# The low halves of the projection's weight tiles move from VectorE to GpSimd

## The chip, the cores and the metric

The kernel runs on one core of a Trainium2 chip. The metric is the device time of one execution in microseconds (us). The core has TensorE (PE in the profile), VectorE (DVE), ScalarE (ACT), GpSimd (POOL) and SyncE (SP), which run side by side and wait for each other on semaphores. DMAs are issued from SP and ACT in the part that matters here.

## What is computed

The reference is two transformer blocks over a sequence of 1024 tokens with 1024 channels: a block with an mLSTM and pooling mixer and a mixture of experts, then a block with attention and a dense network. The change is in the mixer of the first block:

```
mod = (silu(c) @ ada_w + ada_b).reshape(bsz, 6, dm)
h = rms_norm(x, norm1_g) * (1 + scale_a) + shift_a
proj = h @ w_in
y_m = mlstm_group(u, v, o_pre, i_pre, f_pre from proj, ...)
y_p = pool_group(p from proj, ...)
mix = concatenate([y_m, y_p]) @ w_out
x = x + gate_a * mix
```

A large product is made of three in a reduced format, fp32r: each factor is split into a high half (the value rounded to fp32r) and a low half (the value less the high half), and high x high, low x high and high x low are added up. So each weight tile needs a copy that rounds, and a subtraction.

## The kernel before

The mixer's projection has 17 weight tiles of 128 columns, numbered n = 0 to 16: four of u, one of the two gates, four of o, four of p (the pooling part), four of v. For each tile PE makes two halves of 512 tokens (`product`), each of 8 x 3 matmuls. The tiles pass through two buffers each: `wb` (the loaded tile, `w_in_tile` in the profile), `wbh` (`w_in_high`) and `wbl` (`w_in_low`).

The way of one tile: ACT issues the load of tile n (`weights(n)`), which waits until the low half of tile n - 2 is made. When both halves of product n - 2 are evacuated, ACT makes the high half (`high(n)`, line 536, semaphore `s_hi`). DVE makes the low half (`low(n)`, lines 759 to 761, semaphore `s_lo`). PE waits for it at the head of product n. In ACT's order the load of tile n + 3 stands between the evacuations of the two halves of product n, so a late low half holds back the second evacuation as well.

Beside this runs the modulation. Ten rows of 1024 values (numbered bundles 0 to 9 here) are each made of 8 pieces of `ada_w` or `w_ada`, 512 KB a piece. Seven of a bundle's pieces are loaded by SP into three rotating buffers (in `v_aug`); DVE adds each, scaled by a value per partition, to `mod_acc` (`piece(j)`, line 757); SP issues piece j when DVE is done with piece j - 3. The eighth (`last_piece(b)`, line 300) goes straight to PE, in the sums (lines 1132 and 1135), which PE makes behind the product named by `summed_in`: bundle 4 behind product 8, bundles 7 and 8 behind products 11 and 12. SP's program has the last piece of a bundle behind the third piece of the next one, so it is issued once DVE has done the first piece of that next bundle.

DVE's program goes tile by tile: for tile n the convolution of tile n - 1 (lines 770 and 773, n = 1 to 4), its share of pieces (`quota`), then `low(n + 2)`, then behind n = 6 the gate rows (`gate_rows`, lines 790 to 803, a chain over 4 x 1024 values with two scans), and from n = 11 on the window sums of the pooling part (`window_sums`, lines 823 to 827, g = 0 to 3). A wait of DVE in `low` therefore stands ahead of everything behind it in that order.

At the end of the stage ACT may not evacuate v tiles 2 and 3 (tiles 15 and 16) before the four window sums are done, since they share memory; behind that evacuation in ACT's order stand the evacuations of the pool products (line 584), for which PE waits (line 1069).

POOL makes the statistics of the norm, then waits for the 16 steps of the convolutions, sets two mask rows for the gate rows (lines 446 and 448, semaphore `r_z`), waits for the sums of all bundles, and multiplies the output weights by the gate (`gated_weights`, line 472).

Of the kernel before, what the change touches and what calls it, by code (L numbers as in the profile page):

```python
# [13 lines left out]
F32 = mybir.dt.float32  # L14
# [4 lines left out]
ALU = mybir.AluOpType  # L19
# [111 lines left out]
def mixer(nc, a, sbuf, sem, psum, bank, ident, ones, mhalf, mods, x1_dram, normed_dram, moe_dram, rows_dram, chosen, picks, first_raw, first_in, masks):  # L131
# [5 lines left out]
    with ExitStack() as ctx:  # L137
# [9 lines left out]
        wb = sbuf(ctx, "w_in_tile", [P, 2, KT, P])  # L147
        wbh = sbuf(ctx, "w_in_high", [P, 2, KT, P], F32R)
        wbl = sbuf(ctx, "w_in_low", [P, 2, KT, P], F32R)
# [38 lines left out]
        s_hi, s_lo, mm, ev, cv, pc, z, s_vt, s_vc, s_sl = [sem("x_" + n) for n in  # L188
            ("w_high", "w_low", "proj", "evac", "conv", "pcol", "const", "v_turned", "v_copied", "silu")]
# [56 lines left out]
        NT = len(tiles)  # L246
# [29 lines left out]
        with nc.Block() as block:  # L276
            @block.sync
            def _(sp):
# [11 lines left out]
                def weights(n):  # L290
                    _, _, at = tiles[n]
                    sp.dma_start(wb[:, n % 2], w_in_pk[:, :, at:at + P]).then_inc(wl[n % 2], 16)
# [130 lines left out]
            def _(pool):  # L423
# [16 lines left out]
                for t in range(TT):  # L440
                    pool.wait_ge(s_sq, t + 1)
                    pool.tensor_scalar(stat[:, t, 0:1], stat[:, t, 0:1], 1.0 / D, EPS, ALU.mult, ALU.add).then_inc(s_e, 1)
                    pool.wait_ge(s_e, t + 1)
                    pool.tensor_tensor(stat[:, t, 1:2], stat[:, t, 0:1], mhalf[:], ALU.pow).then_inc(s_rs, 1)
                pool.wait_ge(cv, 4 * HM)
                pool.memset(rr[:, 3, :], 1.0).then_inc(r_z, 1)
                pool.wait_ge(r_z, 1)
                pool.memset(rr[:, 3, 0:S:P], 0.0).then_inc(r_z, 1)

                def decay_log(c):  # L450
                    d = by_head(de[c % 2])
                    pool.wait_ge(d_neg, 16 * (c + 1))
                    if c >= 2:
                        pool.wait_ge(c_st, c - 1)
                    pool.tensor_tensor(d, by_head(negm), pk[:, c, 0, :].unsqueeze(2).to_broadcast([P, HM, P]), ALU.add).then_inc(c_dl, 1)
                    pool.wait_ge(c_dl, 2 * c + 1)
                    pool.affine_select(out=d, in_=d, compare_op=ALU.is_ge, fill=NEG, base=0,
                                       pattern=[[0, HM], [1, P]], channel_multiplier=-1).then_inc(c_dl, 1)
# [27 lines left out]
                for i in range(TT + 2):  # L486
                    n = i - 2
# [246 lines left out]
            def _(dve):  # L734
# [10 lines left out]
                def piece(j):  # L745
                    b, k = divmod(j, DK)
                    l, q = later[b]
                    dve.wait_ge(s_mp[j % 3], 16 * (j // 3 + 1))
                    if k == 0:
                        dve.wait_ge(s_mb[b % 2], 16 * (b // 2 + 2))  # L750
                        if b >= 2:
                            dve.wait_ge(s_ms, b - 1)
                        added = bt[:, b % 2, :]
                    else:
                        dve.wait_ge(s_ma, j)
                        added = acc[:, b % 2, :]
                    dve.scalar_tensor_tensor(acc[:, b % 2, :], spare[:, j % 3, :], csil[:, l, k:k + 1], added, ALU.mult, ALU.add).then_inc(s_ma, 1)

                def low(n):
                    dve.wait_ge(s_hi, n + 1)  # L760
                    dve.tensor_tensor(wbl[:, n % 2], wb[:, n % 2], wbh[:, n % 2].bitcast(F32), ALU.subtract).then_inc(s_lo, 1)  # L761

                def convolve(m):
                    dve.wait_ge(ev, place[m, 1])
                    for j in range(CW):

                        src = uT[:, m, 0:S - j]
                        tap = pcol[:, 4 * (CW - 1 - j) + m:4 * (CW - 1 - j) + m + 1]
                        if j == 0:
                            dve.tensor_scalar(ucT[:, m, :], src, tap, None, ALU.mult).then_inc(cv, 1)  # L770
                        else:
                            dve.wait_ge(cv, 4 * m + j)
                            dve.scalar_tensor_tensor(ucT[:, m, j:], src, tap, ucT[:, m, j:], ALU.mult, ALU.add).then_inc(cv, 1)

                def copy_values(m):
                    for b in range(2):
                        dve.wait_ge(s_vt, 2 * m + b + 1)
                        dve.tensor_copy(vaug[:, 4 * b:4 * b + 4, m, 0:P], bank[4 + b].rearrange("p (t e) -> p t e", e=P)).then_inc(s_vc, 1)
# [33 lines left out]
                def window_sums(g):  # L812
                    win = 2 << g
                    dve.wait_ge(ev, place[first["p"] + g, 1])
                    if g == 0:
                        dve.wait_ge(r_st, 48)
                    else:
                        dve.wait_ge(p_sum, g)
                    src = pp[:, g, :]
                    for j in range(g + 1):  # L820
                        dst = uT[:, 2 + j % 2, :]
                        sh = 1 << j
                        dve.tensor_copy(dst[:, 0:sh], src[:, 0:sh])
                        then(dve.tensor_tensor(dst[:, sh:], src[:, sh:], src[:, 0:S - sh], ALU.add))
                        src = dst
                    then(dve.tensor_tensor(src[:, 0:16], src[:, 0:16], fix[:, g, :], ALU.mult))
                    dve.scalar_tensor_tensor(pp[:, g, :], src, 1.0 / win, pp[:, g, :], ALU.mult, ALU.subtract).then_inc(p_sum, 1)
# [42 lines left out]
                for n in range(NT):  # L870
                    if 1 <= n <= HM:
                        convolve(n - 1)
                    if n == 5:
                        dve.wait_ge(ev, place[first["g"], 1])
                        dve.wait_ge(cv, 4 * HM)
                        dve.scalar_tensor_tensor(rr[:, 0, :], zf, -1.0, zf, ALU.mult, ALU.max).then_inc(r_abs, 1)
                    for j in range(until[n - 1] if n else 3, until[n]):
                        piece(j)
                    if n + 2 < NT:
                        low(n + 2)  # L880
                    if n == 6:
                        gate_rows()
                    if 0 <= n - first["p"] - 2 < HM:
                        window_sums(n - first["p"] - 2)
                    if first["v"] + 1 <= n:
                        copy_values(n - first["v"] - 1)
# [38 lines left out]
                for i in range(TT + 3):  # L925
                    y, n, lg = i - 1, i - 2, i - 3
# [3296 lines left out]
```

## Time and profile before

| | us |
|---|---|
| three runs | 2495.33, 2497.85, 2503.66 |
| median | 2497.85 |
| profiled execution, its own time | 2499.09 |
| its span, first to last instruction | 2497.5 |
| busy in the span: PE / DVE / ACT / POOL | 2400.2 / 1915.3 / 1354.0 / 590.3 |
| mean granted clock of TensorE | 0.990 |

Times in the rows are us from the start of the span. The projection takes about 60 to 300. A matmul of the products starts some 0.23 us behind the one before it; its own duration in the profile (0.39 us) overlaps the next. "Idle before" is time in which the engine had nothing to do, with what ended it. A row with x3 is three instructions with their total time.

### The profile page before, as it was taken

Reading aid. Unit: us, or ns where it says so; the run is one execution under the profiler, and the core shown is the slowest. Engines: PE = TensorE matmul, PEld = TensorE weight load, DVE = VectorE, ACT = ScalarE, POOL = GpSimd, SP = SyncE. Lnnn points to the kernel's source line nnn. Section 1 sums busy time; section 2 is a strip of 40 time slices with the busy share of each in tenths; the row PEclk is TensorE's granted clock in tenths of the full one; section 3 lists DMA queues with packets and bytes.
Section 4 is the critical chain, followed back from the end, with each engine's and each line's share of the span. In section 5 each row is a group of like instructions: output and inputs, shape, how many; then the busy total and the mean of one; then the engine's idle time right before and its main releaser. Section 6 shows DMA issues by size and latency. Waiting matters only on the chain. (4 is left out here: it accounts for less than half of the span.)

```text
span 2497.5 us, 33891 instructions
## 1 busy us (share of the span) xinstructions
PE 2400.2 (96%) x11969; PEld 1979.8 (79%) x11969; DVE 1915.3 (77%) x2471; ACT 1354.0 (54%) x1924; POOL 590.3 (24%) x492
## 2 busy tenths in 40 slices
PE   7999999899999999999989999999999999999999
PEld 4766678678888887886688999997788888878887
DVE  4876668678989989897877888887766666657786
ACT  3243323357777777775676676776434444444332
POOL 2000444143333233332711111110042333400000
PEclk8999999999999999999999999999999999999999
DMA  6778255589878899998521111113332443587864
GB/s 253 237 246 297 102 208 206 227 318 397 336 270 308 307 398 395 411 394 337 193 69 51 52 52 51 52 39 116 129 110 86 152 167 139 188 314 260 304 252 152
DMA packets 181316, 535.36 MB, mean 214 GB/s; under 512 B 17711, under 2 KB 77715, under 8 KB 167881
## 3 DMA queue, kind: packets, MB, share of 16 engines
q1 hardware_dynamic: 147260, 462.82, 50.6%
q0 software_dynamic: 12592, 45.63, 4.8%
q10 hardware_dynamic: 21340, 25.29, 2.9%
q8 instruction: 75, 1.23, 0.2%
q14 instruction: 49, 0.39, 0.1%
HBM read 443.38 MB, written 90.33 MB: 214 GB/s over the span
## 5 line engine op out<-in xcount | busy, mean ns | idle before, releaser
L1766 PE MATMUL psum<-w_high,block_hT_high 128*128 128x512 f32 x576 | 232.5, 404 | 6.9 <-DVE w_low L1384 5.7
L1384 DVE TENSOR_TENSOR w_low<-first_w_up,w_high 128x2048 fp32r<-128x2048 f32 x72 | 186.5, 2628 | 53.1 <-ACT w_high L1378 53.1
L1768 PE MATMUL psum<-w_high,block_hT_low 128*128 128x512 f32 x576 | 225.3, 391 | 0.0
L1767 PE MATMUL psum<-w_low,block_hT_high 128*128 128x512 f32 x576 | 224.8, 390 | 0.0
L1766 PE MATMUL psum<-w_qkv_high,fox_hT_high 128*128 128x384 f32 (+1 forms) x512 | 181.6, 355 | 8.5 <-DVE w_qkv_low L2613 3.4
L1384 DVE TENSOR_TENSOR w_low<-first_w_gate,w_high 128x2048 fp32r<-128x2048 f32 x74 | 168.6, 2282 | 19.6 <-ACT w_high L1378 19.4
L1766 PE MATMUL psum<-w_mlp_out_high,hidden_part_high 128*128 128x512 f32 x448 | 174.5, 390 | 3.3 <-DVE hidden L4011 1.8
L1480 POOL TENSOR_TENSOR block_out<-block_out,late_rows 128x1024 f32<-128x1024 f32 x35 | 92.7, 2648 | 359.6 <-ACT block_out L1644 359.6
L1378 ACT ACTIVATE w_high<-first_w_gate 128x2048 fp32r<-128x2048 f32 x74 | 141.2, 1912 | 65.4 <-DMA first_w_gate<-in_w_expert_gate 61.6
L1767 PE MATMUL psum<-w_mlp_out_low,hidden_part_high 128*128 128x512 f32 x448 | 174.3, 389 | 0.0
L1768 PE MATMUL psum<-w_mlp_out_high,hidden_part_low 128*128 128x512 f32 x448 | 174.3, 389 | 0.0
L1768 PE MATMUL psum<-w_qkv_high,fox_hT_low 128*128 128x384 f32 (+1 forms) x512 | 173.7, 339 | 0.0
L1767 PE MATMUL psum<-w_qkv_low,fox_hT_high 128*128 128x384 f32 (+1 forms) x512 | 173.7, 339 | 0.0
L1766 PE MATMUL psum<-mix_hT_high,w_in_high 128*128 128x512 f32 x400 | 163.0, 408 | 3.6 <-DVE w_in_low L761 2.1
L1384 DVE TENSOR_TENSOR w_low<-first_w_down,w_high 128x2048 fp32r<-128x2048 f32 x70 | 156.8, 2277 | 2.4 <-ACT w_high L1378 2.4
L1767 PE MATMUL psum<-mix_hT_low,w_in_high 128*128 128x512 f32 x400 | 157.6, 394 | 0.0
L3763 ACT ACTIVATE hidden_part_high<-hidden_part 128x1024 fp32r<-128x1024 f32 x54 | 57.2, 1060 | 175.8 <-PE psum L1768 171.6
L1766 PEld LDWEIGHTS psum<-w_high,block_hT_high 128*128 128x128 f32 x576 | 108.4, 188 | 42.2 <-DVE w_low L1384 19.2
L1378 ACT ACTIVATE w_high<-first_w_down 128x2048 fp32r<-128x2048 f32 x70 | 130.5, 1915 | 19.5 <-DMA first_w_down<-in_w_expert_down 12.8
L1378 ACT ACTIVATE w_high<-first_w_up 128x2048 fp32r<-128x2048 f32 x72 | 133.9, 1915 | 0.6 <-DMA first_w_up<-in_w_expert_up 0.6
L1768 PEld LDWEIGHTS psum<-w_high,block_hT_low 128*128 128x128 f32 x576 | 108.1, 188 | 23.9
L1767 PEld LDWEIGHTS psum<-w_low,block_hT_high 128*128 128x128 f32 x576 | 108.3, 188 | 20.9 <-issue 0.2
(524 smaller groups left out, 6732.3 us busy)
## 6 DMA issues: line engine op xcount, KB each, us to landing
first_w_gate<-in_w_expert_gate SPq DMA_DIRECT2D x32, 2048.0 KB, 10.0
first_w_up<-in_w_expert_up SPq DMA_DIRECT2D x32, 2048.0 KB, 10.4
first_w_down<-in_w_expert_down SPq DMA_DIRECT2D x31, 2048.0 KB, 10.5
w_mlp_out_quarters<-in_w_mlp_out SPq DMA_DIRECT2D x78, 512.0 KB, 7.0
hidden_part<-hidden_parts SPq DMA_DIRECT2D x54, 512.0 KB, 4.4
v_aug<-in_w_ada SPq DMA_DIRECT2D x48, 512.0 KB, 5.1
expert_rows<-block_out POOLq DMA_DIRECT2D x34, 512.0 KB, 8.3
v_aug<-in_ada_w SPq DMA_DIRECT2D x32, 512.0 KB, 4.8
```

The source lines that it names most:

```text
L1378: act.activation(wh[:, par, half], raw[kind][:, half], ACT.Copy).then_inc(s_wh, 1)
L1384: dve.tensor_tensor(wl[:, par, half], raw[kind][:, half], wh[:, par, half].bitcast(F32), ALU.subtract).then_inc(s_wl, 1)
L1480: pool.tensor_tensor(ob[:, u, :], ob[:, u, :], grow, ALU.mult).then_inc(s_om, 1)
L1766: pe.matmul(out, sh, mh, start=start, stop=False)
L1767: pe.matmul(out, sh, ml, start=False, stop=False)
L1768: return pe.matmul(out, sl, mh, start=False, stop=stop)
L3763: act.activation(sph[u][:, ij], h_split(gc, ij), ACT.Copy).then_inc(q_sh, 1)
```

## The change

The low halves of tiles 2 to 16 are written into POOL's program and taken out of DVE's; those of tiles 0 and 1 stay on DVE. In POOL's program tiles 2 to 6 stand ahead of the wait for the convolutions and the mask rows, 7 to 16 behind them, and all ahead of the wait for the sums and of `gated_weights`. PE's, ACT's and SP's programs and all semaphores are the same.

```diff
@@ gpsimd
                     pool.tensor_tensor(stat[:, t, 1:2], stat[:, t, 0:1], mhalf[:], ALU.pow).then_inc(s_rs, 1)
+                def low(n):
+                    pool.wait_ge(s_hi, n + 1)
+                    pool.tensor_tensor(wbl[:, n % 2], wb[:, n % 2], wbh[:, n % 2].bitcast(F32), ALU.subtract).then_inc(s_lo, 1)
+
+                pool.wait_ge(s_lo, 2)
+                for n in range(2, 7):
+                    low(n)
                 pool.wait_ge(cv, 4 * HM)
                 pool.memset(rr[:, 3, :], 1.0).then_inc(r_z, 1)
                 pool.wait_ge(r_z, 1)
                 pool.memset(rr[:, 3, 0:S:P], 0.0).then_inc(r_z, 1)
+                for n in range(7, NT):
+                    low(n)
@@ vector
                     for j in range(until[n - 1] if n else 3, until[n]):
                         piece(j)
-                    if n + 2 < NT:
-                        low(n + 2)
                     if n == 6:
                         gate_rows()
```

POOL between the statistics of the norm and the output weights, before:

```order
L444 TENSOR_TENSOR x_stat<-x_stat,minus_half 128x1
L446 MEMSET yT 4x1024
L448 MEMSET yT 4x8
L475 MEMSET v_aug 128x32
L472 TENSOR_TENSOR mod_acc<-mod_acc,w_in_tile 128x1024 x2
L472 TENSOR_TENSOR mod_bias<-mod_bias,w_in_tile 128x1024 x2
```

and now:

```order
L444 TENSOR_TENSOR x_stat<-x_stat,minus_half 128x1
L447 TENSOR_TENSOR w_in_low<-w_in_tile,w_in_high 128x1024 x5
L453 MEMSET yT 4x1024
L455 MEMSET yT 4x8
L447 TENSOR_TENSOR w_in_low<-w_in_tile,w_in_high 128x1024 x10
L484 MEMSET v_aug 128x32
L481 TENSOR_TENSOR mod_acc<-mod_acc,w_in_tile 128x1024 x2
```

Fifteen subtractions of 128x1024 came in, five ahead of the mask rows and ten between them and the output weights.

DVE around the gate rows, with the modulation pieces (`mod_acc`) of tiles 5 to 7, before:

```order
L757 SCALAR_TENSOR_TENSOR mod_acc<-v_aug,c_silu,mod_acc 128x1024 x6
L761 TENSOR_TENSOR w_in_low<-w_in_tile,w_in_high 128x1024
L757 SCALAR_TENSOR_TENSOR mod_acc<-v_aug,c_silu,mod_bias 128x1024
L757 SCALAR_TENSOR_TENSOR mod_acc<-v_aug,c_silu,mod_acc 128x1024 x5
L761 TENSOR_TENSOR w_in_low<-w_in_tile,w_in_high 128x1024
L790 SCALAR_TENSOR_TENSOR yT<-gate_rows,yT 4x1024
```

and now:

```order
L766 SCALAR_TENSOR_TENSOR mod_acc<-v_aug,c_silu,mod_acc 128x1024 x6
L766 SCALAR_TENSOR_TENSOR mod_acc<-v_aug,c_silu,mod_bias 128x1024
L766 SCALAR_TENSOR_TENSOR mod_acc<-v_aug,c_silu,mod_acc 128x1024 x5
L799 SCALAR_TENSOR_TENSOR yT<-gate_rows,yT 4x1024
```

Low halves 7 and 8 left; the gate rows follow the pieces directly.

DVE between window sums 2 and 3 (`yT`), before:

```order
L826 TENSOR_TENSOR yT<-yT,pool_fix 128x16
L827 SCALAR_TENSOR_TENSOR yT<-yT 128x1024
L761 TENSOR_TENSOR w_in_low<-w_in_tile,w_in_high 128x1024
L823 COPY yT<-yT 128x1
L824 TENSOR_TENSOR yT<-yT 128x1023
```

and now:

```order
L835 TENSOR_TENSOR yT<-yT,pool_fix 128x16
L836 SCALAR_TENSOR_TENSOR yT<-yT 128x1024
L832 COPY yT<-yT 128x1
L833 TENSOR_TENSOR yT<-yT 128x1023
```

The low half of tile 16, and with it DVE's wait for its high half, no longer stands between the two window sums.

## Rows read from the trace of the kernel before

**Rows 1.** Busy time in stretches of 20 us: us, busy (instructions), clock, DMA share, GB/s.
```profile
...
100.00:120.00 20.00, 19.28 (x89) 14.50 (x88) 18.68 (x17) 5.52 (x9) 0.00 (x0) 1.00 0.74 238
...
160.00:180.00 20.00, 16.03 (x65) 10.59 (x63) 16.82 (x16) 7.99 (x9) 0.00 (x0) 0.91 0.51 171
...
200.00:220.00 20.00, 20.00 (x88) 15.02 (x87) 13.63 (x11) 5.29 (x8) 0.00 (x0) 1.00 0.93 323
...
```

**Rows 2.** Waits of PE from 60 to 300: line, for whom, total, times, longest.
```profile
...
PE psum L1132 <- DMA v_aug<-in_w_ada: 6.5, 3, 2.8
PE psum L1069 <- ACT yT L584: 2.1, 1, 2.1
PE psum L1766 <- DVE w_in_low L761: 2.1, 1, 2.1
PE psum L1132 <- DMA v_aug<-in_ada_w: 1.2, 1, 1.2
...
```

**Rows 3.** PE in order of time: start, us, engine, line, names, shapes, count, idle before.
```profile
...
175.57 1.87 PE L1132 MATMUL psum<-v_aug,c_silu 128*1 128x512 f32 x4 [2.81 <-DMA v_aug<-in_w_ada]
...
180.95 0.50 PE L1766 MATMUL psum<-mix_hT_high,w_in_high 128*128 128x512 f32 x1 [2.11 <-DVE w_in_low L761]
...
193.64 1.03 PE L1132 MATMUL psum<-v_aug,c_silu 128*1 128x512 f32 x4
...
196.30 0.48 PE L1766 MATMUL psum<-mix_hT_high,w_in_high 128*128 128x512 f32 x1
...
207.37 1.03 PE L1132 MATMUL psum<-v_aug,c_silu 128*1 128x512 f32 x4
...
209.19 0.50 PE L1766 MATMUL psum<-mix_hT_high,w_in_high 128*128 128x512 f32 x1
...
```

**Rows 4.** DVE in order of time around the low halves and the gate rows.
```profile
...
80.72 1.23 DVE L761 TENSOR_TENSOR w_in_low<-w_in_tile,w_in_high 128x1024 fp32r<-128x1024 f32 x1 [0.71 <-ACT w_in_high L536]
...
126.27 1.23 DVE L761 TENSOR_TENSOR w_in_low<-w_in_tile,w_in_high 128x1024 fp32r<-128x1024 f32 x1 [2.29 <-ACT w_in_high L536]
...
152.28 4.06 DVE L757 SCALAR_TENSOR_TENSOR mod_acc<-v_aug,c_silu,mod_acc 128x1024 f32<-128x1024 f32 x3 [4.23 <-DMA v_aug<-in_w_ada]
156.26 1.22 DVE L761 TENSOR_TENSOR w_in_low<-w_in_tile,w_in_high 128x1024 fp32r<-128x1024 f32 x1
157.39 1.21 DVE L790 SCALAR_TENSOR_TENSOR yT<-gate_rows,yT 4x1024 f32<-4x1024 f32 x1
...
169.24 1.28 DVE L757 SCALAR_TENSOR_TENSOR mod_acc<-v_aug,c_silu,mod_acc 128x1024 f32<-128x1024 f32 x1
...
```

**Rows 5.** SP in order of time: the last piece of bundle 4.
```profile
...
170.92 0.43 SPq L300 DMA_DIRECT2D v_aug<-in_w_ada  x1
...
```

**Rows 6.** POOL, then DVE, in order of time, 261 to 280.
```profile
...
261.69 4.72 POOL L472 TENSOR_TENSOR mod_acc<-mod_acc,w_in_tile 128x1024 f32<-128x1024 f32 x2 [7.97 <-DMA mod_acc<-in_w_out]
266.37 6.71 POOL L472 TENSOR_TENSOR mod_bias<-mod_bias,w_in_tile 128x1024 f32<-128x1024 f32 x2
...
266.25 1.25 DVE L761 TENSOR_TENSOR w_in_low<-w_in_tile,w_in_high 128x1024 fp32r<-128x1024 f32 x1 [5.03 <-ACT w_in_high L536]
...
267.48 3.36 DVE L824 TENSOR_TENSOR yT<-yT 128x1023 f32<-128x1023 f32 x1
270.87 2.23 DVE L823 COPY yT<-yT 128x2 f32<-128x2 f32 x1
...
279.21 1.22 DVE L827 SCALAR_TENSOR_TENSOR yT<-yT 128x1024 f32<-128x1024 f32 x1
...
```

**Rows 7.** POOL writing fp32r, in the stage after the mixer.
```profile
...
496.52 1.74 POOL L1457 TENSOR_TENSOR block_tokens<-block_onehot,token_id 128x384 fp32r<-128x384 f32 x1 [5.76 <-DVE block_onehot L1701]
...
```

**Rows 8.** ACT in order of time: the high half of tile 9, and its late evacuation.
```profile
...
162.41 1.05 ACT L536 ACTIVATE w_in_high<-w_in_tile 128x1024 fp32r<-128x1024 f32 x1
...
280.61 0.60 ACT L562 ACTIVATE yT<-psum 128x512 f32<-128x512 f32 x1 [13.05 <-DVE yT L827]
...
```

**Rows 9.** POOL in order of time: the mask rows.
```profile
...
120.06 0.94 POOL L446 MEMSET yT<- 4x1024 f32 x1 [64.38 <-DVE ucT L773]
...
```

## Prediction

> **What bounds the kernel now.** I read the page first: one core, span 2497.5 us, its own run 2499.09 us, TensorE (PE) busy 96%, and the chain that ended last is PE nearly throughout. So time is won or lost only where PE waits. The change touches one stretch, the projection of the mixer, some 60 to 300 us from the start. The table of stretches [rows 1] shows PE busy nearly all of 100:120 but 16.03 of 20 us in 160:180, at a mean granted clock of 0.91, with the DMA engines at 0.51 there against 0.74. VectorE (DVE) is busy 18.68 of 20 us in 100:120. The list of waits [rows 2] then names what PE lacks: 6.5 us (3 times) and 1.2 us for the DMA of a modulation piece ("last piece", used by the sums), 2.1 us once for a low half made by DVE, 2.1 us once for ScalarE's (ACT's) evacuation of a pool product at the end of the stage. The low halves as such cost PE only one wait of 2.11 us.
>
> PE in order of time [rows 3]: the sums of bundle 4 stand at 175.57 after 2.81 us of waiting for the piece, and product 9 begins at 180.95 after another 2.11 us for its low half. Sums take 209.19 - 207.37 = 1.82 us where PE is warm; here 180.95 - 2.11 - 175.57 = 3.27 us. Product 9 lasts 193.64 - 180.95 = 12.69 us against 207.37 - 196.30 = 11.07 for product 10, so 1.6 us go to the half clock (1.2 of 2.4 GHz) that the idle time left behind.
>
> Why the last piece is late: DVE [rows 4] makes low 8 at 156.26, then the gate rows from 157.39 to 169.24, and only then the first piece after them, which ends at 170.52; SP issues the last piece at 170.92 [rows 5], 4.65 us before PE has it. That chain, DVE to SP to DMA to PE, is what the change moves.
>
> **Step 1, the work leaves DVE.** 15 low halves (tiles 2 to 16) go. One is 1.22 us, and costs DVE 157.39 - 156.26 = 1.13 us in a row [rows 4]. DVE also loses the waits that it makes only for a high half: 0.71 us before low 2 and 2.29 before low 6 [rows 4], and 5.03 before low 16 [rows 6]. The same 15 go to GpSimd (POOL), which did almost nothing there. One multiplication of this shape takes POOL 4.72 / 2 = 2.36 us with DVE silent [rows 6]. The output type (fp32r) isn't in that row; the only POOL row that writes it took 1.74 us for 384 columns [rows 7], beside a DVE instruction. By columns that bounds it at 1.74 x 1024 / 384 = 4.6 us; the lower end is 2.3. I take 2.36, since the inputs and shape are those of that row. Either is far inside the time that a product lasts, so the low half is ready before PE wants it: the high half of tile 9 ends at 162.41 + 1.05 = 163.46 [rows 8], its low half would at 165.8, PE wants it near 179.
>
> **Step 2, the price: the two engines exclude each other.** Where POOL multiplies at 266.37 (two, 6.71 us instead of 4.72), DVE's addition at 267.48 takes 3.36 us instead of 1.22, and a copy of two columns at 270.87 takes 2.23 us [rows 6]. So each POOL instruction holds DVE's next one back by 3.36 - 1.22 = 2.14 us if DVE has work, and by nothing if DVE waits for a DMA; DVE gets one instruction in between. A low half that cost DVE 1.13 us now costs it 0 to 2.14.
> The Trainium skill, "SBUF — State Buffer", section "Who interferes with whom", says the same as a rule: a VectorE instruction with two SBUF inputs and a GpSimd one that reads SBUF need one port, and whoever comes second blocks for the whole instruction. By that rule the change could be a loss on DVE wherever DVE is busy; the trace agrees, with the 2.14 us above.
>
> Up to 127 us DVE is the busy one. Five low halves (2 to 6): 5 x (2.14 - 1.13) = +5.0 us, less the waits 0.71 + 2.29 = -3.0, leaves +2.0; DVE's short waits for pieces take up part of it, I take +1.2. From 127 to 157 the pieces wait for their loads (4.23 us before the one at 152.28 [rows 4]); low 7 and 8 leave, -2.26, and the POOL low 8 (ready at about 149.3) falls into that very wait; but pieces that wait for loads give only part of this back. I take -1.9 with half a block of +0.9 for low 7, net -1.0. Low 9 (163.46) falls into the gate rows, two-input instructions in a chain: +2.14. Some of it overlaps the instruction already running: +1.1 to +2.14. Together the last piece of bundle 4 is issued 1.2 - 1.0 + 1.1 = +1.3 us later. Bounds: -3 (all blocks hidden, only the saved waits) to +9.2 (8 full blocks, 8 x 2.14 = 17.1, less 7 x 1.13 = 7.9, nothing else given back).
>
> **Step 3, what PE gets.** At product 9: the sums begin 1.3 us later, 176.9, last 3.3, product 9 begins at 180.1 instead of 180.95: -0.8. The wait for the low half (2.11) goes, the wait for the piece grows. Less idle time, so perhaps less half clock: of the 1.6 us I count half, -0.8 (0 to -1.6). At the sums of the two later bundles that wait, PE loses the other 6.5 - 2.81 = 3.7 us [rows 2, 3]. There DVE is busy only 13.63 of 20 us [rows 1]: it waits for loads itself, so 1.13 us less work per tile brings little: -0.3 (-3.7 if these waits go, +1.3 if the delay of the last piece is carried on).
>
> **Step 4, the end of the stage.** Window sum 3 ends at 279.21 + 1.22 = 280.43 [rows 6]. Before it DVE waited from 261.22 to 266.25, 5.03 us, for the last high half, then made low 16; then POOL's multiplications by the gate blocked it three times. ACT waited 13.05 us for it [rows 8], and PE 2.1 us for ACT [rows 2]. In the new order, window sum 3 follows window sum 2 at once, at 261.2. It took 280.43 - 267.4 = 13.0 us, 6.6 without the three blocks; with two blocks (low 15 or 16 and one multiplication) it is 10.9, so it is done by 272.1 even if nothing before it is earlier; ACT then evacuates tile 15 as soon as PE has made it. The 2.1 us go: -2.1. Cover gone? POOL now starts to multiply the output weights by the gate after low 16, at about 268.6 instead of 261.69: five times 2.36 to 3.36 us (6.71 / 2), done by 281 to 286. ACT takes them up only when product 16 is done, two half products (11.07 us) and more behind the 280.61 of [rows 8]: hidden. The mask rows, a memset of 0.94 us at 120.06 [rows 9], come after low 6, about 129, and are needed by the gate rows at 157: hidden.
>
> **Sum.** -0.8 - 0.8 - 0.3 - 2.1 = -4.0 us on 2499.09: 2495.1. That execution is 1.24 us above the median of the three runs (2497.85), which would be 2493.9; I say 2494.5. Behind the mixer nothing changes, and PE's chain carries the shift to the end.
>
> **Rivals.**
> A, forecast: as above, 2494.5.
> B, the blocks hide nearly all: then the last piece comes 2.2 us earlier (low 7 and 8), the 2.11 goes, the half clock goes (1.6), the later waits halve (-1.9), one of the slow sums there becomes a warm one (3.27 - 1.82 = -1.5), and step 4 stays: -2.2 - 2.1 - 1.6 - 1.9 - 1.5 - 2.1 = -11.4, so 2487. For it: DVE is idle a third of the time once past the gate rows [rows 1]. Against: in 100:120 it is busy 93%, and the gate rows have no gaps.
> C, slower: the port. If DVE is held by full blocks up to the gate rows and gets nothing back, the last piece is 9.2 us late. Product 9 then begins 9.2 - 2.1 = 7.1 us later; less the 2.1 of step 4 that is +5.0. The later loads follow the same DVE and keep the delay, and the waits behind them grow by as much as they are now (+3.7): +8.7, 2507. It decides from a delay of the last piece above 4.2 us (2.11 + 2.1). A POOL instruction of 4.6 us leads here too. For it: 18.68 of 20 [rows 1]; against: DVE waits for loads between 127 and 157, where delay is taken up.
> D, the change does little: the piece chain gets as late as the low half was (+2.1) and step 4 is the only gain: 2497.
> The Trainium skill, "GPSIMD Engine Reference", section "3.1 Elementwise — side-by-side cycle accounting", puts a two-input GpSimd operation at about twice VectorE's time and keeps elementwise work on VectorE. The rows say 2.36 against 1.22. By that rule alone the move is wrong; it becomes a loss only through the blocks, which is C.
>
> **Numbers.** A 0.55, D 0.15, B 0.18, C 0.12. A change of 0.3% (7.5 us) is about what a measurement of this kernel can tell from none; the three runs shown differ by 8.3 us. A and D lie within it, 0.70, with 0.03 of B and 0.02 of C: same 0.75, faster 0.15, slower 0.10. The range 2487 to 2502 leaves out C and the best of B; A's own is 2490 to 2498.
>
> **What the new profile would show.** Step 1: w_in_low written by POOL 15 times at 2.4 to 3.5 us, no wait of PE for it. Step 2: DVE pieces, convolutions and gate rows with single durations of 2.5 to 3.5 us in place of 1.2, about one for each POOL low; the gate rows ending at 170 to 171. Step 3: the last piece of bundle 4 issued near 172, PE's wait for it 3 to 5 us. Step 4: no wait of PE for ACT at the pool products, window sum 3 done before 273. I am wrong if PE's waits for pieces rise above 12 us in the stage (then C), or vanish (B), or if a POOL low takes over 4 us alone.

## The result

The changed kernel took 2508.59 us (median of 9 runs, 2494.24 to 2516.26), the kernel before 2497.85 us (9 runs, 2492.85 to 2504.61). The ratio is 1.0040, 95% interval 1.0023 to 1.0057: slower by 0.4%, a difference clear of zero, where 2494.5 and "no change to be told" were forecast. The time is just above rival C's 2507.

The profiled execution of the changed kernel took 2507.42 us, its span 2505.8, so 8.3 us more than before on both. The place is the projection. As its length I take the time from DVE's low half of token tile 5 to the first query/key matmul of PE: 299.83 - 63.05 = 236.8 us before, 308.83 - 61.44 = 247.4 changed (both rows are below). That is +10.6; the execution began that stretch 1.6 us earlier and the rest of the span is 0.7 us shorter.

Waits of PE in the changed kernel from 60 to 300 (line, for whom, total, times, longest), beside [rows 2]:

```profile
PE psum L1139 <- DMA v_aug<-in_w_ada: 12.3, 4, 3.5
PE psum L1139 <- DMA v_aug<-in_ada_w: 6.2, 2, 4.5
```

The waits for a low half and for ACT's evacuation are gone, as forecast. The waits for last pieces grew from 7.7 to 18.5 us.

Busy time in stretches of the changed kernel (columns as in [rows 1]):

```profile
100.00:120.00 20.00, 15.48 (x63) 10.18 (x62) 18.47 (x14) 4.29 (x7) 2.82 (x1) 0.83 0.65 214
160.00:180.00 20.00, 17.52 (x78) 14.17 (x76) 18.44 (x15) 8.37 (x10) 2.47 (x1) 1.00 0.43 142
200.00:220.00 20.00, 20.00 (x88) 14.74 (x87) 13.22 (x10) 5.42 (x8) 3.09 (x1) 0.95 0.82 277
```

In 100:120, where PE was busy 19.28 of 20 us before, it is now busy 15.48, at a granted clock of 0.83. In 160:180 it is busier than before (17.52 us, 16.03 in [rows 1]): there the gain at product 9 shows. In 200:220 it is busy throughout, as before, at a transfer share of 0.82 instead of 0.93. The first of the three stretches is ahead of the gate rows and of every wait of PE that the forecast reckoned with.

PE in order of time in the changed kernel, beside [rows 3]: the sums of bundles 1, 4, 5, 7 and 8, the heads of products 4, 9 and 14, and the first query/key matmul:

```profile
...
112.10 1.87 PE L1139 MATMUL psum<-v_aug,c_silu 128*1 128x512 f32 x4 [4.52 <-DMA v_aug<-in_ada_w]
...
116.99 0.48 PE L1773 MATMUL psum<-mix_hT_high,w_in_high 128*128 128x512 f32 x1
...
180.22 1.03 PE L1139 MATMUL psum<-v_aug,c_silu 128*1 128x512 f32 x4 [2.71 <-DMA v_aug<-in_w_ada]
...
182.53 0.80 PE L1773 MATMUL psum<-mix_hT_high,w_in_high 128*128 128x512 f32 x1
...
197.82 1.20 PE L1139 MATMUL psum<-v_aug,c_silu 128*1 128x512 f32 x4 [3.04 <-DMA v_aug<-in_w_ada]
...
229.73 1.87 PE L1139 MATMUL psum<-v_aug,c_silu 128*1 128x512 f32 x4 [3.50 <-DMA v_aug<-in_w_ada]
...
247.26 1.87 PE L1139 MATMUL psum<-v_aug,c_silu 128*1 128x512 f32 x4 [3.10 <-DMA v_aug<-in_w_ada]
...
264.78 0.50 PE L1773 MATMUL psum<-mix_hT_high,w_in_high 128*128 128x512 f32 x1
...
308.83 1.06 PE L1192 MATMUL psum<-ucT,query_key 128*128 128x128 f32 x8
...
```

The first wait is 4.52 us at bundle 1. The sums and transposes behind it run at the half clock (granted 0.50 in 112:116, against 1.00 in 109:114 before): from 112.10 to the next product 4.89 us, against 112.70 - 109.29 = 3.41 before. Then come bundles 3 (1.63, before 1.17), 4 (2.71, before 2.81), 5 (3.04, before none), 7 (3.50, before 2.66) and 8 (3.10, before 1.08).

To see why bundle 1 is late, DVE, SP and PE in the kernel before: the start of the stretch, a convolution, a piece, the issue of the last piece of bundle 1, its sums and the product behind them, DVE's first instruction on the gates' tile, the head of product 14 and the end of the stretch:

```profile
...
63.05 1.22 DVE L743 TENSOR_TENSOR mix_hT_low<-psum,mix_hT_high 128x1024 fp32r<-128x1024 f32 x1
...
82.65 3.92 DVE L773 SCALAR_TENSOR_TENSOR ucT<-yT,param_cols,ucT 128x1023 f32<-128x1023 f32 x3
...
91.42 1.28 DVE L757 SCALAR_TENSOR_TENSOR mod_acc<-v_aug,c_silu,mod_acc 128x1024 f32<-128x1024 f32 x1 [0.87 <-DMA v_aug<-in_ada_w]
...
102.83 0.43 SPq L300 DMA_DIRECT2D v_aug<-in_ada_w  x1
...
109.29 1.03 PE L1132 MATMUL psum<-v_aug,c_silu 128*1 128x512 f32 x4
...
112.70 0.48 PE L1766 MATMUL psum<-mix_hT_high,w_in_high 128*128 128x512 f32 x1
...
127.42 1.20 DVE L876 SCALAR_TENSOR_TENSOR yT<-gate_rows 4x1024 f32<-4x1024 f32 x1
...
253.42 0.50 PE L1766 MATMUL psum<-mix_hT_high,w_in_high 128*128 128x512 f32 x1
...
299.83 1.06 PE L1185 MATMUL psum<-ucT,query_key 128*128 128x128 f32 x8
...
```

and in the changed kernel DVE at the same places and around the gate rows, then SP's issues of the last pieces of bundles 1, 4, 5 and 7:

```profile
...
61.44 1.22 DVE L752 TENSOR_TENSOR mix_hT_low<-psum,mix_hT_high 128x1024 fp32r<-128x1024 f32 x1
...
79.40 5.94 DVE L782 SCALAR_TENSOR_TENSOR ucT<-yT,param_cols,ucT 128x1023 f32<-128x1023 f32 x3
...
85.26 3.42 DVE L766 SCALAR_TENSOR_TENSOR mod_acc<-v_aug,c_silu,mod_bias 128x1024 f32<-128x1024 f32 x1
...
93.33 1.28 DVE L766 SCALAR_TENSOR_TENSOR mod_acc<-v_aug,c_silu,mod_acc 128x1024 f32<-128x1024 f32 x1 [1.87 <-DMA v_aug<-in_ada_w]
...
95.31 5.95 DVE L782 SCALAR_TENSOR_TENSOR ucT<-yT,param_cols,ucT 128x1023 f32<-128x1023 f32 x3
...
129.61 1.22 DVE L885 SCALAR_TENSOR_TENSOR yT<-gate_rows 4x1024 f32<-4x1024 f32 x1 [2.84 <-ACT gate_rows L578]
...
159.98 1.21 DVE L799 SCALAR_TENSOR_TENSOR yT<-gate_rows,yT 4x1024 f32<-4x1024 f32 x1
...
168.54 2.78 DVE L807 TENSOR_SCALAR yT<-yT 4x1024 f32<-4x1024 f32 x1
...
105.64 0.43 SPq L300 DMA_DIRECT2D v_aug<-in_ada_w  x1
...
175.61 0.43 SPq L300 DMA_DIRECT2D v_aug<-in_w_ada  x1
...
190.37 0.43 SPq L300 DMA_DIRECT2D v_aug<-in_w_ada  x1
...
222.28 0.43 SPq L300 DMA_DIRECT2D v_aug<-in_w_ada  x1
...
```

Three convolution steps together take 5.94 and 5.95 us instead of 3.92, and a piece 3.42 instead of 1.28: three blocks of 2.0 to 2.1 us, one for each of the POOL subtractions of low 2, 3 and 4, which start at 79.23, 84.69 and 95.48. SP issues the last piece of bundle 1 at 105.64 - 61.44 = 44.2 us into the stretch instead of 102.83 - 63.05 = 39.8, and PE has it 6.46 us after the issue.

The rows also show which piece sets these issues. SP's program has the last piece of a bundle behind the load that waits for the bundle's own seventh piece (for bundle 4 the one at 169.24 in [rows 4]; the next bundle's first piece, with `mod_bias` among its inputs, starts only at 170.44), not behind DVE's first piece of the next bundle. The times read from the rows stay the same.

### The profile page after: what moved, and what is told of

It is laid out like the page before. It is cut to its first block and busy times, and to the rows that moved or that the text cites. A ratio compares the mean times of both kernels' runs of the same rounds, so it can differ in the third digit from the quotient of the medians.

```text
span 2505.8 us, 33892 instructions
## 1 busy us (share of the span) xinstructions
PE 2402.1 (96%) x11969; PEld 1978.4 (79%) x11969; DVE 1915.9 (76%) x2456; ACT 1354.6 (54%) x1924; POOL 636.0 (25%) x507
## 6 DMA issues: line engine op xcount, KB each, us to landing
first_w_gate<-in_w_expert_gate SPq DMA_DIRECT2D x32, 2048.0 KB, 10.3
first_w_up<-in_w_expert_up SPq DMA_DIRECT2D x32, 2048.0 KB, 10.2
```

## The experiments

Each kernel from memset_low on ran in five rounds beside the kernel before. In the four series (that of the result and three more) the median of the kernel before was 2497.85, 2498.29, 2499.67 and 2498.49 us; kernels of different series are best compared by their ratios. "Issue 1", "issue 4" and "issue 8" are the issues of the last pieces of bundles 1, 4 and 8 in the profiled execution, in us from the start of the stretch; "stretch" is its length. Each kernel has one profiled execution, so how far a stretch repeats is not measured; I don't read differences of under 2 us in it. The rest of the span, behind and ahead of the stretch, varies more: from 2253.4 us (after_b1) to 2267.8 (two_tiles), in no order that follows the edits. So a difference of a few us in the time need not lie in the stretch. Up to bundle 1 the traces repeat: issue 1 is 39.8 or 39.9 in all eight kernels that leave low halves 2 to 6 on DVE without extra POOL work.

| kernel | median us | ratio to before (95%) | issue 1 | issue 4 | issue 8 | stretch |
|---|---|---|---|---|---|---|
| before | 2498 | | 39.8 | 107.9 | 168.6 | 236.8 |
| changed | 2508.6 | 1.0040 (1.0023 to 1.0057) | 44.2 | 114.2 | 178.3 | 247.4 |
| memset_low | 2494.6 | 0.9991 (0.9977 to 1.0006) | 36.9 | 105.0 | 166.9 | 236.1 |
| extra_blocks | 2510.8 | 1.0059 (1.0042 to 1.0077) | 45.8 | 117.8 | 180.0 | 250.4 |
| late_tiles | 2499.8 | 1.0011 (0.9996 to 1.0026) | 39.8 | 109.2 | 170.8 | 236.0 |
| early_tiles | 2504.6 | 1.0017 (1.0001 to 1.0034) | 44.2 | 111.7 | 172.2 | 242.2 |
| two_tiles | 2499.1 | 0.9995 (0.9979 to 1.0012) | 39.8 | 108.8 | 170.9 | 236.2 |
| late_tiles_loads | 2497.8 | 0.9986 (0.9970 to 1.0002) | 39.8 | 108.5 | 172.0 | 238.1 |
| early_last | 2503.0 | 1.0030 (1.0013 to 1.0047) | 42.5 | 96.5 | 173.9 | 246.0 |
| after_b1 | 2504.1 | 1.0018 (1.0005 to 1.0032) | 42.7 | 114.0 | 176.2 | 241.5 |
| two_tiles_b4 | 2501.1 | 0.9998 (0.9980 to 1.0016) | 39.9 | 91.7 | 169.7 | 237.6 |
| inter_before | 2495.9 | 0.9993 (0.9981 to 1.0005) | 39.8 | 96.4 | 165.8 | 235.2 |
| inter_two | 2496.4 | 0.9987 (0.9973 to 1.0001) | 39.9 | 96.5 | 167.3 | 234.8 |
| inter_late | 2494.3 | 0.9984 (0.9969 to 0.9998) | 39.8 | 96.8 | 168.2 | 237.0 |

**memset_low: the change without GpSimd's reads.**

```diff
-                    pool.tensor_tensor(wbl[:, n % 2], wb[:, n % 2], wbh[:, n % 2].bitcast(F32), ALU.subtract).then_inc(s_lo, 1)
+                    pool.memset(wbl[:, n % 2].bitcast(F32), 0.0).then_inc(s_lo, 1)
```

> The changed kernel, but GpSimd fills the low halves of tiles 2 to 16 with zero (a memset, which reads nothing) instead of subtracting, so the product lacks that term. Order, semaphores and the early release of the tile buffers stay. Stage length is measured from VectorE's low half of token tile 5 to the first query/key matmul: 236.8 us before, 247.4 changed. Theory P (the port: GpSimd's reads hold VectorE, so the pieces, and with them SP's issue of the last pieces, come late): single durations of pieces and convolutions back at 1.28 us, stage 228 to 234 us, PE's waits for pieces 5 to 10 us (18.5 in the changed kernel), time 2484 to 2493. Theory L (loads: with the tile buffers released earlier, the loads of the w_in tiles collide with those of the pieces): stage stays 244 to 249, time as changed, near 2508.

Measured: 2494.6 us, 14 under the changed kernel; stretch 236.1. A POOL memset and a convolution beside it, a piece, the issue of the last piece of bundle 1, a gate row with one input, then a tile load of ACT, the last piece of bundle 5 and PE's wait for it:

```profile
...
79.94 1.16 POOL L447 MEMSET w_in_low<- 128x1024 f32 x1 [25.21 <-ACT w_in_high L545]
...
80.24 3.92 DVE L782 SCALAR_TENSOR_TENSOR ucT<-yT,param_cols,ucT 128x1023 f32<-128x1023 f32 x3
...
88.82 1.28 DVE L766 SCALAR_TENSOR_TENSOR mod_acc<-v_aug,c_silu,mod_acc 128x1024 f32<-128x1024 f32 x1 [0.68 <-DMA v_aug<-in_ada_w]
...
99.10 0.43 SPq L300 DMA_DIRECT2D v_aug<-in_ada_w  x1
...
161.38 1.53 DVE L807 TENSOR_SCALAR yT<-yT 4x1024 f32<-4x1024 f32 x1
...
179.47 0.55 ACTq L554 DMA_DIRECT2D w_in_tile<-in_w_in  x1
...
181.68 0.96 SPq L300 DMA_DIRECT2D v_aug<-in_w_ada  x1
...
189.63 1.87 PE L1139 MATMUL psum<-v_aug,c_silu 128*1 128x512 f32 x4 [4.77 <-DMA v_aug<-in_w_ada]
...
```

The convolutions are back at 3.92 us and issue 1 stands at 36.9, 7.3 us earlier than in the changed kernel and 2.9 earlier than before. So the loss comes with POOL's reads, as theory P says, and not with the early tile loads, which this kernel has too. But P also asked for 2484 to 2493 and a stretch of 228 to 234, and that missed. DVE is rid of 15 low halves almost free of price (a gate row with one input, the row at 161.38, still takes 1.53 us instead of 0.68), and the median is 3.7 us lower, with an interval from 5.7 us lower to 1.5 higher. In its trace product 9 begins 6.4 us earlier than before (111.52 us into the stretch, before 117.90), and product 14 begins 1.7 us later (192.10, before 190.37): with no block at all, a lead of 6.4 us at the gate rows is spent on waits for pieces behind them. PE waits 4.77 us at bundle 5 for a piece issued at 181.68, 7.95 us before, just behind a tile load.

**extra_blocks: the price alone.** The kernel before with 13 POOL subtractions that nobody needs, for tiles 2 to 6 ahead of the mask rows and for 7 to 14 behind them; DVE still makes every low half:

```diff
+                def block(n):
+                    pool.wait_ge(s_hi, n + 1)
+                    pool.tensor_tensor(sq[64:P, :], hTh[64:P, 0, :].bitcast(F32), hTl[64:P, 0, :].bitcast(F32), ALU.subtract).then_inc(s_junk, 1)
```

> The kernel before, its low halves on VectorE, plus 13 GpSimd subtractions of 64 partitions x 1024 from tensors that don't change, each at the time of the high half of tiles 2 to 14, into an unused place. Theory P: each holds VectorE up to 2.1 us on top of the 1.13 us that it still spends on the low half; stage 248 to 256 us, PE waits at the sums of bundles 1, 4, 7 and 8, time 2509 to 2518. Theory L: nothing is loaded at another time, so stage 236 to 239 and time as before, 2498.

Measured: 2510.8 us, +12.5, stretch +13.6, and waits at bundles 1, 3, 4, 7 and 8, as theory P had it; theory L is out. DVE, POOL and SP in order of time:

```profile
...
82.78 5.93 DVE L786 SCALAR_TENSOR_TENSOR ucT<-yT,param_cols,ucT 128x1023 f32<-128x1023 f32 x3
...
84.27 3.37 POOL L448 TENSOR_TENSOR x_square<-mix_hT_high,mix_hT_low 64x1024 f32<-64x1024 f32 x1 [2.07 <-ACT w_in_high L549]
...
106.86 0.43 SPq L300 DMA_DIRECT2D v_aug<-in_ada_w  x1
...
```

The three steps together are 2.0 us longer than 3.92, although this POOL instruction covers only 64 of 128 partitions.

**late_tiles and early_tiles: the change in two halves.** In late_tiles DVE keeps low 2 to 6, in early_tiles low 7 to 16; POOL's program has the others. DVE's part (the first wait keeps the low halves in their order):

```diff
+                    if n + 2 < NT and n + 2 not in (7, 8, 9, 10, 11, 12, 13, 14, 15, 16):   # (2, 3, 4, 5, 6) in early_tiles
+                        dve.wait_ge(s_lo, n + 2)
+                        low(n + 2)
```

> Low halves 2 to 6 back on VectorE, 7 to 16 on GpSimd. Theory P: the wait of 4.5 us at the sums of bundle 1 and the slow clock behind it go (about 6 us), the waits at the later bundles stay near 2 to 3 us each: stage 238 to 242, time 2499 to 2503. Theory L: the early tile loads are only released a little earlier in either kernel, so the bundle 1 wait stays and the stage is 245 to 248, time 2506 to 2509.

> The other half of the split: low halves 2 to 6 on GpSimd, 7 to 16 on VectorE as before. If the two halves of the change add up (changed kernel 10.3 us over before, late half alone 1.5 over), this one is 6 to 11 us over before: 2504 to 2509. Theory P in its narrow form (the loss is made where VectorE is the busy engine, up to 127 us, and reaches TensorE first at the sums of bundle 1): a wait of 4 to 5 us there, gate rows some 3 to 5 us later than in before, and the wait for low half 9 (2 us) is back. Rival (the loss is the sum of small delays all over, 15 blocks alike): a third of 10.3, 2501 to 2502.

Measured: 2499.8 and 2504.6 us. In late_tiles the wait at bundle 1 is gone, as theory P had it, and its stretch of 236.0 rules theory L out (it is also 2 us below P's range); the late half costs nothing that can be told. The early half costs 4.9 us by the medians of its series, with an interval from 0.2 to 8.5 us. Issue 1 of early_tiles is 44.25, that of the changed kernel 44.20. PE in early_tiles in order of time, the sums of bundle 1 and product 9:

```profile
...
110.76 1.87 PE L1147 MATMUL psum<-v_aug,c_silu 128*1 128x512 f32 x4 [4.55 <-DMA v_aug<-in_ada_w]
...
182.46 0.80 PE L1781 MATMUL psum<-mix_hT_high,w_in_high 128*128 128x512 f32 x1 [4.26 <-DVE w_in_low L775]
...
```

The wait at bundle 1 is the changed kernel's, the gate rows start 3.8 us later than before, and the wait for low half 9 is back: the three signs of P's narrow form. The time alone decides nothing here: +4.9 us is under the 6 to 11 asked for, and an even share for each block (a third of 10.3, 3.4 us) lies within the interval.

The two halves don't add up in the traces. At issue 4 they have +1.3 and +3.8 us and the whole has +6.3; at issue 8 they have +2.2 and +3.6 and the whole +9.7. So some 4 us at issue 8 come only with both. In the times the intervals leave room for a plain sum (0.11% and 0.17% against 0.40%). Why both together cost more is not shown; that the late blocks meet a DVE that is already behind is an argument.

**two_tiles: only the two low halves that somebody waited for** (9 and 16 on POOL).

> Only low halves 9 and 16 on GpSimd, the two for which an engine waited in before (TensorE 2.11 us at product 9, VectorE 5.03 us ahead of window sum 3). Theory P: the gains of the change with 2 of 15 blocks: the waits of 2.1 and 2.1 us go, stage 4 to 5 us under before, 2492 to 2495. Theory S (the loads set the pace behind the gate rows, so what TensorE gains it waits for at the next bundles): the 2.1 us at product 9 comes back as a wait for the pieces of bundles 5 to 8 and only the 2.1 us at the end stays, 2495 to 2498.

Measured: 2499.1 us, no gain. Waits of PE in this kernel:

```profile
PE psum L1141 <- DMA v_aug<-in_w_ada: 12.3, 5, 4.5
...
PE psum L1141 <- DMA v_aug<-in_ada_w: 1.2, 2, 0.8
...
PE psum L1775 <- DVE w_in_low L769: 0.8, 1, 0.8
```

The waits for ACT and for low half 9 are gone (0.8 us at low 10 came), and the waits for pieces went from 7.7 to 13.5 us. Theory S predicted the form. Its 2 us of gain at the end are in the trace: product 14 begins 1.8 us later than before and the stretch ends 0.6 us shorter, so 2.4 us come back behind product 14. The median is too coarse to show them (the interval is -5.2 to +3.0 us).

**late_tiles_loads: late_tiles with the tile loads held back.**

```diff
                     evac(n, 0)
-                    if n + 3 < NT:
-                        weights(n + 3)
...
                     evac(n, 1)
+                    if n + 3 < NT:
+                        weights(n + 3)
```

> The late half of the change (7 to 16 on GpSimd) with the load of tile n + 3 issued behind the evacuation of the second half of product n instead of ahead of it, some 5 us later, near where the late low halves put it in before. Theory L in a smaller form (the wait for the last piece of bundle 5, absent in before and 3.0 to 5.8 us in every kernel whose low half 9 is early, comes from the tile load issued right ahead of it): that wait goes, its load lands in under 6 us, time 2495 to 2498. Theory S (the loads as a whole are the limit there): the wait stays at 2 us or more or turns up at the next bundle, time 2499 to 2501.

Measured: 2497.8 us. The wait at bundle 5 is gone, as theory L in its smaller form says, but bundles 4, 6, 7 and 8 wait 3.85, 3.35, 2.85 and 1.39 us, and the wait at bundle 6 is larger than in late_tiles (2.83 us), as theory S says. The difference of 2 us to late_tiles is within both intervals. Not settled between the two.

**early_last, after_b1, two_tiles_b4: last pieces issued two pieces earlier**, for all bundles, for bundle 1 and for bundle 4:

```diff
-                        if sent % DK == 2 and sent > DK:
+                        if sent % DK == 0 and sent >= DK:
...
-                        if sent % DK == 2 and sent > DK:
+                        if sent > DK and sent % DK == (0 if sent // DK - 1 in (1,) else 2):   # (4,) in two_tiles_b4
```

> The changed kernel, with SP issuing the last piece of each bundle two pieces earlier (behind the first piece of the next bundle's loads instead of the third). Theory P: PE waited for the issue of these loads; bundle 4's now goes out ahead of the gate rows. PE's waits for pieces fall from 18.5 to under 6 us, stage 230 to 236, time 2487 to 2497, faster than both. Theory L: the loads as a whole are late, so the wait only moves to the other operand or to the next pieces; waits 14 us or more, stage 243 to 248, time 2504 to 2509.

> The changed kernel with the last piece of bundle 1 alone issued two pieces earlier. Theory P in the form that TensorE's wait at bundle 1 (4.5 us, plus 3 us of slow clock) is what carries the loss: 4 to 7 us under the changed kernel, 2502 to 2505. Theory S (VectorE's delay carries the loss through the pieces and their loads, TensorE only shows it): the wait at bundle 1 falls below 2 us and turns up behind it, time within 2 us of the changed kernel, 2507 to 2510.

> As the kernel with only low halves 9 and 16 on GpSimd, and SP issues the last piece of bundle 4 alone two pieces earlier, ahead of the gate rows (near 157 instead of 171). TensorE's wait of 2.8 us for it goes. Theory P: 3 to 5 us under the kernel with the two tiles alone, 2488 to 2491. Theory S: the pieces behind the gate rows start when they did, the loads set the pace, and the gain comes back as waits at bundles 5, 7 and 8: within 1.5 us of the two tiles alone.

Measured: 2503.0, 2504.1 and 2501.1 us. early_last is not faster than before, a miss for theory P; its median is 5.6 us under that of the changed kernel, but the ratios 1.0030 and 1.0040 don't separate the two. PE's waits for pieces come to 20.1 us and the stretch to 246.0, both inside what theory L asked for (14 us or more, 243 to 248), and its time is 1 us below L's range. The pieces for VectorE are now the late ones. Waits of PE in it:

```profile
PE psum L1139 <- DMA v_aug<-in_w_ada: 10.8, 3, 5.8
PE psum L1142 <- DVE mod_acc L766: 5.1, 2, 4.2
PE psum L1139 <- DMA v_aug<-in_ada_w: 4.2, 2, 2.4
```

after_b1 came 4.5 us under the changed kernel, which P had, though the two intervals overlap (up to 1.0032, from 1.0023). Its wait at bundle 1 only fell to 3.39 us and its issue 1 only from 44.2 to 42.7, so it doesn't show that PE's wait there is what carries the loss. In two_tiles_b4 the wait at bundle 4 is gone and 6.17 us stand at bundle 5, the form of theory S; its median is 2.0 us over two_tiles, where S allowed 1.5, which is within the noise.

**inter_before, inter_two, inter_late: four pieces between the links of the gate rows**, in the kernel before, in two_tiles, in late_tiles_loads (the pieces behind the gate rows are four fewer in return):

```diff
                     links[0] += 1
+                    if links[0] in (1, 2, 3, 5):
+                        piece(until[6] + (1, 2, 3, 5).index(links[0]))
                     dve.wait_ge(r_ch, links[0])
```

> The kernel before, low halves on VectorE; four modulation pieces (34 to 37) are made between the first links of the gate rows instead of behind them. The loads of the next pieces and of the last piece of bundle 4 then go out some 8 to 10 us earlier, while the DMA engines are otherwise half idle (0.51 of 160:180). Theory S (behind the gate rows the loads set the pace, so only loads that start earlier help): the waits for pieces of bundles 4, 7 and 8 (6.5 us in before) nearly go, stage 5 to 9 us shorter, time 2490 to 2494. Theory T (TensorE's own work sets the pace and only its single waits count): the wait of bundle 4 goes (-3), the gate rows end 5 us later and delay ScalarE and low half 9, within 2 us of before.

> As the last one, with low halves 9 and 16 on GpSimd. Low half 9, behind more pieces in VectorE's order, would be later still; on GpSimd it is ready at 166. Theory S: the 2 us at product 9 and 2 us at the end count now that the loads have room: 3 to 4 us under the kernel with the pieces alone, 2487 to 2491. Theory T: the two tiles give what they gave alone, nothing: 2498 to 2500.

> Pieces between the gate rows, low halves 7 to 16 on GpSimd, tile loads behind the second evacuation. Ten blocks of 2.1 us against ten low halves of 1.1 us on VectorE, which is idle a third of the time there. Theory S: as the kernel with two tiles or 1 us better, 2486 to 2491. If the blocks cost there as well (changed kernel against the memset: late half about 5 us), 2492 to 2495.

Measured: 2495.9, 2496.4 and 2494.3 us. DVE in inter_late in order of time, gate rows and pieces in turn:

```profile
...
155.84 1.27 DVE L781 SCALAR_TENSOR_TENSOR mod_acc<-v_aug,c_silu,mod_acc 128x1024 f32<-128x1024 f32 x1
...
157.03 2.27 DVE L817 TENSOR_TENSOR_SCAN yT<-yT 4x1024 f32<-4x1024 f32 x1
...
169.75 0.68 DVE L824 TENSOR_SCALAR yT<-yT 4x1024 f32<-4x1024 f32 x1
...
```

Issue 4 comes 11 us earlier than before, issue 8 only 0.4 to 2.8 us. So most of the lead is gone four bundles later, and the gains of 5 to 9 us that theory S asked for missed. inter_late is the only kernel whose interval lies under 1 (0.9984, 0.9969 to 0.9998): about 4 us better than before and 14 better than the change. It is a small gain, it is one interval of thirteen, and its stretch of 237.0 us doesn't show where it would come from.

## Why the prediction was wrong

**The sum, term by term.** The profiled executions give each term of the sum its measured size. Times are those at which a product begins, from the start of the stretch: product 9 at 182.53 - 61.44 = 121.09 us (before 180.95 - 63.05 = 117.90), product 14 at 264.78 - 61.44 = 203.34 (before 253.42 - 63.05 = 190.37). Product 9 lasts 197.82 - 3.04 - 182.53 = 12.25 us (before 12.69).

| term | forecast, us | measured, us |
|---|---|---|
| up to the head of product 9 (step 3) | -0.8 | +3.2 |
| product 9 itself, the half clock (step 3) | -0.8 | -0.4 |
| behind it, to the head of product 14 (step 3, the later bundles) | -0.3 | +10.2 |
| from product 14 to the end (step 4) | -2.1 | -2.4 |
| sum | -4.0 | +10.6 |

**Step 1 held.** POOL's low halves took 2.35 to 3.67 us (2.36 alone was taken), the shortest of them with the fp32r output that the row for 2.36 lacked, and PE waited for none.

**Step 2 is the step that failed first: "Together the last piece of bundle 4 is issued ... +1.3 us later".** Measured: 114.2 against 107.9, +6.3 us. The block itself was right: 2.0 to 2.1 us, 2.14 taken. Its balance was not, in any of its three parts. Up to DVE's first instruction on the gates' tile (127.42 before, 129.61 changed) 1.2 us were taken, and it is +3.8. From there to the gate rows (157.39 and 159.98) -1.0 were taken, and it is +0.4. In the gate rows 1.1 were taken, and it is +2.1, a full block (the row at 168.54), which the forecast had as its upper bound.

The first part failed for three reasons.

- The blocks were set off against the low halves one to one. But a POOL subtraction starts when the high half is ready, and the DVE one stood behind the pieces of that tile. Ahead of issue 1 stand three blocks (low 2, 3, 4) and only two removed low halves (2, 3): 3 x 2.07 - 2 x 1.13 - 0.71 = +3.2 us.
- The waits for loads were to take up part of the delay. Ahead of issue 1 they grew, from 1.90 + 0.87 to 2.20 + 1.87 us: +1.3. Together that is +4.5, measured +4.4. The three kernels 39.8 / 36.9 / 44.2 (before, memset_low, changed) show the split: taking the low halves away is worth -2.9 there, POOL's reads +7.3.
- The 2.29 us that DVE lost before low 6 were counted as won. But the next thing that DVE needs is the evacuation of the gates' tile by ACT. In memset_low DVE waits 5.07 us for it, and starts 124.42 - 62.17 = 62.25 us into the stretch, only 2.1 us earlier than before, although five low halves have left its program by then. In the changed kernel it waits 2.84 us and starts at 68.17, 5.9 us later than in memset_low, as much as PE is late behind bundle 1. So the delay went from DVE over SP, the load, PE and ACT back to DVE.

**Step 3 left bundle 1 out, and had the later bundles wrong.** I looked for the effect where PE already waited (bundle 4 and behind). The last piece of bundle 1 was issued at 102.83 and its sums stood at 109.29, 6.46 us later. Where PE waited for this piece it landed 5.6 to 7.1 us after its issue (6.46 in the changed kernel, 7.08 in two_tiles, which has the same issue 1 as before and waits 0.77 us). So there was less than 1 us of slack, and no row of the waits could say so, because PE arrived just in time. The wait of 4.52 us and the slow clock behind it make the first 5.9 us: the next product begins 116.99 - 61.44 = 55.55 us into the stretch, before 112.70 - 63.05 = 49.65. The gain at product 9 came, so that PE is only 3.2 us late there.

The largest miss is the term for the later bundles: -0.3 was taken, and PE lost 10.2 us behind product 9, 4.7 of them at bundle 5, 0.8 at bundle 7, 3.7 at bundle 8 and 1.1 behind it. The way there stood in the range of the step, "+1.3 if the delay of the last piece is carried on"; it was carried on and grew, from +6.3 at issue 4 to +9.7 at issue 8. Not all of this is the price of the blocks: memset_low, which has none of them, spends 6.4 + 1.7 = 8.1 us between the heads of products 9 and 14. late_tiles and two_tiles do the like: product 9 begins 2.2 and 0.9 us earlier than before there, product 14 1.5 and 1.8 us later. In none of the three was what PE gained up to product 9 kept.

**Step 4 held.** ACT no longer waits for window sum 3 and PE no longer for ACT (no such row among the waits above). From the head of product 14 to the end of the stretch it is 299.83 - 253.42 = 46.41 us before and 308.83 - 264.78 = 44.05 changed, -2.4 against -2.1 forecast. It is 44.05 in nine of the ten kernels in which POOL makes low half 16 (45.90 in early_last), and 45.99 to 48.25 in the four in which DVE makes it. In the changed kernel these 2.4 us don't cover the 13.0 lost ahead of them.

**The rivals.** C had the mechanism, the place ("held up to the gate rows") and the sign; it was given 0.12. That its 2507 is so close is partly luck: its terms were +7.1 at product 9, -2.1 at the end and +3.7 behind, and measured were +3.2, -2.4 and +9.8 (10.2 less the 0.4 in product 9). Its bound of +9.2 at the last piece was met at bundle 8 (+9.7), not at bundle 4. What spoke against it, that the waits for loads between 127 and 157 would take delays up, did not happen (+3.8 ahead of them, +4.2 behind them); the DMA share is 0.85 and 0.84 in 120:140 and 140:160 of the kernel before. B is refuted by memset_low: with every block gone the median is 3.7 us lower, not 11.4. The forecast of -4.0 is close to that kernel's median; but its trace has other terms (-6.4, +8.1, -2.4), so that is a coincidence of the sum.

**What stays open.** How the 5.3 us between issue 1 (+4.4) and issue 8 (+9.7) arise is only bounded: +2.2 of the whole at issue 8 come with the late blocks alone and +3.6 with the early ones alone, and no run separates the rest further.

## What to carry to other kernels

Before work is moved between DVE and POOL, count on both sides of each deadline, not per stage: a POOL instruction blocks at the time its input is ready, the DVE instruction that it replaces stood where the program put it. And read the slack of the waits that are not there: a consumer that arrives a landing time after the issue of its load is on the path although no wait shows. In these kernels a wait taken from PE behind the gate rows came back at the next loads (two_tiles, two_tiles_b4, memset_low), and even loads that started 11 us earlier left at most 2.8 us four bundles later.

## What the runs showed of the hardware

- A POOL subtraction over 64 partitions holds DVE as long as one over 128: 2.0 to 2.1 us (extra_blocks; changed kernel). It also holds a DVE instruction with a single input over 4 partitions (168.54: 2.78 us; 0.68 in inter_late).
- A POOL memset of the same tile (0.95 us alone) left the two-input DVE instructions beside it as they were (three convolution steps in 3.92 us from 80.24, memset_low). A DVE instruction with one input took 1.53 us beside it instead of 0.68 (161.38).
- The load of a last piece (512 KB) reached PE 4.6 us after its issue at bundle 4 of the changed kernel (180.22 - 175.61; DMA share 0.43 in 160:180), and 7.5 us after it at bundles 5 and 7 (197.82 - 190.37, 229.73 - 222.28; 0.82 in 200:220).
